# Six gate and up places and eight down places, four weight loads under way, and the last two pairs of experts interleaved

## What is computed

```python
def _hierarchical_moe(xt, w_rg, b_rg, w_re, b_re, w_gate, w_up, w_down):
    ...
    combine = jnp.sum(jax.nn.one_hot(expert_id, N_EXPERTS, dtype=jnp.float32)
                      * (g1 * g2)[..., None], axis=1).astype(xt.dtype)
    y = jnp.zeros_like(xt)
    for e in range(N_EXPERTS):
        he = jax.nn.silu(xt @ w_gate[e]) * (xt @ w_up[e])
        y = y + combine[:, e:e + 1] * (he @ w_down[e])
    return y
...
        x = x + y.reshape(B, T, D)
    return _rmsnorm(x, final_norm)
```

## Time and profile before

| | us |
|---|---|
| runs, median of 3 | 1471.9 |
| runs, lowest and highest | 1466.81, 1473.19 |
| profiled execution | 1470.25 |
| its span (first to last instruction) | 1468.4 |
| PE, DVE, ACT, POOL busy | 1337.8, 662.8, 505.2, 572.6 |
| weight loads (SP), DMA share of the span on its queue | 35.5% |

### The profile page before, as it was taken

One profiled execution on the slowest core, in us unless ns is written; L12 is line 12 of the kernel. 1 busy time (PEld: TensorE's weight loads), 2 busy tenths in 40 slices (PEclk: granted clock), 3 DMA queues, 4 the chain that ended last, 5 costly groups with the idle time before them and its releaser, 6 DMA issues. The chain is left out here.

```text
span 1468.4 us, 20026 instructions
## 1 busy us (share of the span) xinstructions
PE 1337.8 (91%) x7696; PEld 955.2 (65%) x7696; DVE 662.8 (45%) x1346; ACT 505.2 (34%) x970; POOL 572.6 (39%) x531
## 2 busy tenths in 40 slices
PE   4999999989999899798998999999999889999855
PEld 3767767778878776576888876677767733333222
DVE  5456953257722679624761413443444611111115
ACT  3312333356632423335662433544442111111002
POOL 2113687334444437953436403543342311111125
PEclk9999999999999999889999999999999799999988
DMA  8672111130022311120003212211036959999993
GB/s 336 269 283 100 44 44 44 43 129 1 2 90 90 113 58 58 44 86 15 1 2 102 72 58 86 87 58 44 29 143 242 368 210 394 358 371 371 376 346 153
DMA packets 42652, 210.06 MB, mean 143 GB/s; under 512 B 7271, under 2 KB 9703, under 8 KB 33328
## 3 DMA queue, kind: packets, MB, share of 16 engines
q1 hardware_dynamic: 34336, 195.11, 35.5%
q0 software_dynamic: 5760, 10.27, 1.9%
q10 hardware_dynamic: 2448, 3.21, 0.7%
HBM read 201.98 MB, written 17.30 MB: 149 GB/s over the span
## 5 line engine op out<-in xcount | busy, mean ns | idle before, releaser
L425 POOL TENSOR_TENSOR wlo<-raw,whi 128x1024 fp32r<-128x1024 f32 x57 | 139.4, 2447 | 107.0 <-ACT whi L413 73.6
L3260 PE MATMUL ps<-gu,XT 128*64 128x512 f32 x608 | 136.7, 595 | 6.9 <-DVE XT L3360 4.2
L853 PE MATMUL ps<-hxh,whi 128*128 128x512 f32 x304 | 131.6, 433 | 5.7 <-ACT whi L413 5.7
L853 PE MATMUL ps<-hxh,wlo 128*128 128x512 f32 x304 | 124.0, 408 | 13.8 <-POOL wlo L425 13.8
L1115 DVE SCALAR_TENSOR_TENSOR z<-glu,small,z 128x798 f32<-128x798 f32 (+1 forms) x120 | 129.1, 1127 | 0.7
L853 PE MATMUL ps<-hxl,whi 128*128 128x512 f32 x304 | 122.4, 403 | 0.0
L3260 PEld LDWEIGHTS ps<-gu,XT 128*64 128x64 f32 x608 | 46.5, 137 | 84.1 <-issue 73.1
L1618 POOL TENSOR_SCALAR P<-P,stat 128x768 f32<-128x768 f32 (+1 forms) x80 | 65.5, 821 | 84.6 <-DVE stat L1580 83.5
L3285 PE MATMUL ps<-dn,heT 128*64 128x512 f32 x304 | 78.5, 626 | 21.8 <-issue 12.4
L1462 PE MATMUL ps<-kT,qT 96*128 96x256 f32 (+1 forms) x432 | 91.7, 348 | 3.8 <-ACT P L1516 2.1
L1516 ACT ACTIVATE P<-ps,stat 128x768 f32<-128x768 f32 (+1 forms) x80 | 65.1, 814 | 63.2 <-DVE stat L1573 62.6
(11 more groups left out here) (844 smaller groups left out, 3173.3 us busy)
## 6 DMA issues: line engine op xcount, KB each, us to landing
gu<-in_w_gu_dram SPq DMA_DIRECT2D x32, 2048.0 KB, 10.0
raw<-in_w_in_dram SPq DMA_DIRECT2D x66, 512.0 KB, 3.4
dn<-in_w_dn_dram SPq DMA_DIRECT2D x32, 1024.0 KB, 7.6
wgate<-in_w_mod_dram SPq DMA_DIRECT2D x16, 1024.0 KB, 8.5
raw<-in_w_out_dram SPq DMA_DIRECT2D x24, 512.0 KB, 3.3
wmod<-in_w_mod_dram SPq DMA_DIRECT2D x4, 2048.0 KB, 13.6
ybuf<-zero SPq DMA_DIRECT2D x1, 4096.0 KB, 12.0
yin<-ybuf SPq DMA_DIRECT2D x4, 1024.0 KB, 10.0
```

The source lines that it names most:

```text
L425: e.tensor_tensor(K.lo[i][:, :], K.raw[i % 2][:, :], K.hi[i][:, :].bitcast(F32), ALU.subtract).then_inc(*q.up("lo", i))
L853: p = e.matmul(s[0:m, o:o + n], a, K.h[l, v][x][:, k, :], start=k == 0 and part == 0 and x == 0, stop=end)
L3260: m = e.matmul(s[o, :], x[:, k, o], gu[:, k, :], start=k == 0, stop=k == KT - 1, skip_group_check=True)
```

## The change

- There are 6 gate and up places and 8 down places, and the list of first loads has 14 entries, the last five (gu3, gu4, dn6, gu5, dn7) after the attention output is done.
- A load waits for the load four ahead of it, not two.
- Pair 14's up goes into the interleaved loop: up 14, down 13, (far jobs), turn of pair 15's rows, turn of he; after the loop up 15, down 14, the first sums, down 15. Its results still become y parts and not scatters. The second XT and the held bank are gone.
- yin, y parts, owner matrices and row2 lie in other weight places that are free by then; far jobs use another he buffer.

```diff
--- before.py
+++ after.py
@@ -24,7 +24,7 @@
-N_GU, N_DN = 7, 6
+N_GU, N_DN = 6, 8
@@ -317,7 +317,7 @@
-      + [(f"dn{i}", 8 * kb, 130, 199) for i in range(N_DN)]
+      + [(f"dn{i}", 8 * kb, 130 if i < 6 else 131, 199) for i in range(N_DN)]
@@ -2550,7 +2550,7 @@
-    last_walk(S, loads=loads, more_loads=lambda: experts_load(S, 4))
+    last_walk(S, loads=loads, more_loads=lambda: experts_load(S, 5))
@@ -2891,7 +2891,7 @@
-    first = ["gu0", "gu1", "dn0", "dn1", "gu2", "dn2", "dn3", "dn4", "dn5", "gu3", "gu4", "gu5", "gu6"]
+    first = ["gu0", "gu1", "dn0", "dn1", "gu2", "dn2", "dn3", "dn4", "dn5", "gu3", "gu4", "dn6", "gu5", "dn7"]
@@ -2914,14 +2914,14 @@
-    return after("last") + [("x_out", 1, T2 - 1, 1)] * (w == "gu" and x > 2)
+    return after("last") + [("x_out", 1, T2 - 1, 1)] * (x > (2 if w == "gu" else 5))
...
-        for s in q(*weight_free(w, x), *([("w", *EXPERT_LOADS[i - 2])] if i > 1 else [])):
+        for s in q(*weight_free(w, x), *([("w", *EXPERT_LOADS[i - 4])] if i > 3 else [])):
@@ -2934,14 +2934,14 @@
-    last = PAIRS - 3
-    E.w_gu, E.w_dn = weight_place(K, "gu", 2 * PAIRS), weight_place(K, "dn", 2 * last)
-    E.row2 = sb("row2", [128, D], F32, f"dn{(2 * last + 1) % N_DN}")
-    E.yin = [sb(f"yin{t}", [128, 2, D], F32, f"gu{(2 * last + t // 2) % N_GU}", 8192 * (t % 2)) for t in range(T2)]
-    E.x2 = sb("XT2", [128, KT, 128], F32, f"dn{(2 * last + 1) % N_DN}", 4096)
...
+    last = NE - 6
+    at = lambda w, x: f"{w}{x % (N_GU if w == 'gu' else N_DN)}"
+    E.w_gu, E.w_dn = weight_place(K, "gu", last), weight_place(K, "dn", last)
+    E.yin = [sb(f"yin{t}", [128, 2, D], F32, at("gu", last + t // 2), 8192 * (t % 2)) for t in range(T2)]
+    E.parts = [[sb(f"y{j}{p}", [128, D], F32R, at("dn", (last + 1, last - 2)[j]), 4096 * c) for c, p in enumerate("hl")] for j in range(2)]
+    E.owner = [sb(f"own{j}", [128, T2, 128], F32R, at("dn", last - 1), 2048 * j) for j in range(4)]
+    E.row2 = sb("row2", [128, D], F32, "Y")
@@ -3077,36 +3077,13 @@
-    for i in range(PAIRS - 2):
...
-    lower(i)
-    second_stored(i)
-
     def far(n):
...
-        upward(job, "XT", 0)
-        downward(job, 0, y)
+        upward(job, "XT", 1)
+        downward(job, 1, y)
@@ -3115,13 +3092,37 @@
-    guarded(everyone, farther(0), all_far)
+    p, last = PAIRS - 2, PAIRS - 1
+    turned(("first", 0), ("xg", 0), "XT")
+    first_gather(2)
+    for i in range(last):
+        job, job2 = ("first", i), ("second", i)
+        upward(job, "XT", 0)
+
+        def more_up():
+            turned(job2, "xg2", "XT")
+            upward(job2, "XT", 1 + i % 2)
+        if i < p:
+            guarded(numbers, crowded(i), more_up)
+        load(loads_of("gu", i))
+        if i < p:
+            turned(("first", i + 1), ("xg", (i + 1) % 2), "XT")
+        if i + 1 < p:
+            second_gather(i + 1)
+        first_gather(i + 3)
+        if i:
+            lower(i - 1)
+            second_stored(i - 1)
+        if i == p:
+            guarded(everyone, farther(0), all_far)
+            turned(("first", last), ("xg", 1), "XT")
+        turn_up(job, 0, free("heT"))
+        free.set(("he", 0), ev("he_turned", job))
...
-    free.at["part", 0], free.at["part", 1] = free(("Y", 0)) + free(("Y", 1)), end
+    free.at["part", 0] = free.at["part", 1] = end
@@ -3156,18 +3157,14 @@
     owner(0, "pool", end)
     owner(2, "pool", end)
-    turned(("first", p), ("xg", 0), "XT")
-    upward(("first", p), "XT", 0)
-    downward(("first", p), 0, None, 0)
-    free.at["x2"] = end
-    turned(("first", last), ("xg", 1), "x2")
-    hold_up(("first", last))
+    upward(("first", last), "XT", 0)
+    down(("first", p), None, 0, free(("part", 0)))
+    free.set("heT", ev("down", ("first", p), 1))
     guarded(numbers, crowded(p), lambda: own_second(p, 1))
...
     taken_in(0)
-    upward(("first", last), "x2", 0)
     begin_sum(0)
     begin_sum(1)
```

More of the change, by code:

```diff
@@ L2936, in experts_buffers @@
     E.heT = sb("heT", [128, 2, 128], F32, "he", 3072)
-    last = PAIRS - 3
-    E.w_gu, E.w_dn = weight_place(K, "gu", 2 * PAIRS), weight_place(K, "dn", 2 * last)
-    E.row2 = sb("row2", [128, D], F32, f"dn{(2 * last + 1) % N_DN}")
-    E.yin = [sb(f"yin{t}", [128, 2, D], F32, f"gu{(2 * last + t // 2) % N_GU}", 8192 * (t % 2)) for t in range(T2)]
-    E.x2 = sb("XT2", [128, KT, 128], F32, f"dn{(2 * last + 1) % N_DN}", 4096)
-    place = f"gu{2 * PAIRS % N_GU}"
-    E.parts = [[sb(f"y{j}{p}", [128, D], F32R, *((place, 4096 * c) if j else ("Y", 4096 * (1 - c)))) for c, p in enumerate("hl")] for j in range(2)]
-    E.owner = [sb(f"own{j}", [128, T2, 128], F32R, place, 8192 + 2048 * j) for j in range(4)]
+    last = NE - 6
[5 more added lines that the diff above has]
+    E.row2 = sb("row2", [128, D], F32, "Y")
     E.ms2, E.rs2 = K.stat[:, 64:68], K.stat[:, 72:76]
@@ L3007, in lists, with experts_walk @@
     return [("list",), *[("h2d", t) for t in range(T2)]]
-def experts_walk(S, engine, empty2=nothing, gather=nothing, load=nothing, turn_x=nothing, hold_up=nothing, up=nothing, turn_up=nothing, down=nothing,
+def experts_walk(S, engine, empty2=nothing, gather=nothing, load=nothing, turn_x=nothing, up=nothing, turn_up=nothing, down=nothing,
                  scatter=nothing, stored=nothing, far_load=nothing, rows_in=nothing, owner=nothing, add=nothing, to_x=nothing, rows_sum=nothing,
@@ L3079, in lower @@
         load(loads_of("dn", i))
-    turned(("first", 0), ("xg", 0), "XT")
-    first_gather(2)
-    for i in range(PAIRS - 2):
-        job, job2 = ("first", i), ("second", i)
-        upward(job, "XT", 0)
[L3086 to L3099, removed]
-    lower(i)
-    second_stored(i)
     def far(n):
@@ L3117, in all_far @@
             guarded(everyone, farther(n), lambda: far(n))
-    guarded(everyone, farther(0), all_far)
+    p, last = PAIRS - 2, PAIRS - 1
[23 more added lines that the diff above has]
+        free.set(("he", 0), ev("he_turned", job))
     end = free("heT")
-    p, last = PAIRS - 2, PAIRS - 1
     second_gather(p)
     rows_in(end, free(("Y", 0)) + free(("Y", 1)))
-    free.at["part", 0], free.at["part", 1] = free(("Y", 0)) + free(("Y", 1)), end
+    free.at["part", 0] = free.at["part", 1] = end
     for t in range(T2):
@@ L3131, in own_second @@
         turned(job, "xg2", "XT")
-        upward(job, "XT", 0)
-        downward(job, 0, None, 1)
+        upward(job, "XT", 1)
+        downward(job, 1, None, 1)
         for t in range(T2):
@@ L3246, in turn_x @@
                     m.then_inc(*q.up(*ev("x_turned", job, c)))
-    def hold_up(job):
-        held[job] = K.bk.hold(*ev("he", job))
     def up(job, xt, j, free):
-        s, before = held[job] if job in held else take(*ev("he", job))
-        x, ws = E.x2 if xt == "x2" else E.XT, weights_of(K, E, job)
+        s, before = take(*ev("he", job))
+        x, ws = E.XT, weights_of(K, E, job)
         n = 128 // len(ws)
@@ L3262, in up @@
                     m.then_inc(*q.up(*ev("up", job)))
-        if job in held:
-            K.bk.release(*ev("he", job))
     def turn_up(job, j, free):
@@ L3305, in add @@
                 K.bk.release(*name)
-    experts_walk(S, "pe", turn_x=turn_x, hold_up=hold_up, up=up, turn_up=turn_up, down=down, add=add)
+    experts_walk(S, "pe", turn_x=turn_x, up=up, turn_up=turn_up, down=down, add=add)
 def experts_act(S):
@@ L3314, in turn_x @@
     def turn_x(job, buf, xt, free):
-        x = E.x2 if xt == "x2" else E.XT
+        x = E.XT
         for w in q(ev("x_turned", job, 1), *free):
```

## The result

| | before | after |
|---|---|---|
| median, us | 1469.36 (1466.41 to 1473.19, 4 runs) | 1448.64 (1447.80 to 1451.45, 4 runs) |
| ratio | | 0.9861, 95% interval 0.9829 to 0.9892 |
| profiled execution, span | 1470.25, 1468.4 | 1447.80, 1446.0 |

The change takes 20.7 us off, where the forecast had 12 and a time of 1459 us. In the traced executions the spans differ by 22.4 us.

The account below looks back on a forecast made before the run. From 1195 us the expert weights' DMA stream, then the work after its last landing, was taken to bound the kernel. Gains of 7 us from the rate and 5 from the order gave 1459 us, range 1451 to 1467.

Parts of the forecast that it names:

- What bounds: Expert stage, from 1195 us: the weights still to come set the end, then the work after the last of them.
- W: Expert stage: the landing of the last weight, dated at 1429 us before and forecast at 1422 after.
- Places, 0: Weight places, 7 and 6 becoming 6 and 8: nothing won or lost, the stretch before 1195 staying as it is.
- Four under way, 7.1 us: Weight stream from 1195: four loads under way raise DMA share from 0.96 to 0.99, winning 7.1 us, bounds 0 and 9.4.
- Rival (3): Weight stream and end: all comes back, share 0.998 and no slow clock, yin loads earlier: 1453 us; chance 0.10.
- The rule on HBM: Weight stream: HBM side binds at about 358 GB/s a core, so four under way would win 0; the prediction held it contradicted.
- The order, 5 us: Last two pairs: up 14 before down 13 and up 15 before down 14 win about 5 us.
- Down 15 at W + 11: Last pair: its down matmuls start at 1433.0 instead of 1444.87, 11 us after the last weight instead of 15.9.
- rival (4): Expert stage, result buffer Y0: rows starve as scatters slow beside more queued weights; slower, 1491 us; chance 0.05.
- The yin loads, covered by 1.4 us: End: yin loads wait for pair 13's scatter; VectorE's 1.2 us take-in ends at 1430.6, copy of he due at 1432.
- Slow clock, 1.5 us: Up 15, after TensorE's wait for gu31: a lower granted clock adds 1.5 us, bounds 0 to 7.
- From the last down to the end, 23.5 us: End of the kernel: the same work in the same order follows the last down, 23.5 us.

Follow-up runs that it names:

- E1: The kernel before with each weight load waiting for the load four ahead instead of two, old places and order kept: 1457.65 us, ratio 0.9921.
- E7: The changed kernel with the old order of the last two pairs put back, new places and four loads under way kept: 1458.27 us, ratio 0.9943.
- E2: The changed kernel with two weight loads under way again instead of four, new places and order kept: 1463.65 us, ratio 0.9956.
- E4: The changed kernel with two Y result buffers used in turn by the first jobs instead of one: 1445.99 us, ratio 0.9845.
- E6: The changed kernel with two Y buffers in turn and six weight loads under way instead of four: 1445.4 us, ratio 0.9847.
- E9: The changed kernel with each weight load as two halves over all 128 partitions, a half waiting for the half three ahead: 1472.65 us, ratio 1.0018.
- E10: The changed kernel with each weight load as two halves over all 128 partitions, a half waiting for the half eight ahead: 1443.31 us, ratio 0.9816.
- E5: The changed kernel with each weight load as two halves of 64 partitions, a half waiting for the half three ahead: 1644.25 us, ratio 1.1199.
- E8: The kernel before with four weight loads under way and two Y buffers used in turn: 1454.85 us, ratio 0.9911.
- E11: The changed kernel with two Y buffers in turn and pair 15's turn of he and down ahead of the first sums: 1445.72 us, ratio 0.9840.
- E12: The changed kernel run again, unedited, in the same series as E9 to E11: 1448.74 us, ratio 0.9852.

## Why the prediction was wrong, point by point

- **What bounds: right.** E1, which changes the gate alone, moves the end by 10 us. The dating of W (1429) holds by the packets too.
- **Places, 0: right.** E7 has them and E1 not, and the two are alike. The share ahead of 1195 was 0.25 (0.23 before), and the first load after it began at 1194.4 (1195 before).
- **Four under way, 7.1 us with bounds of 0 and 9.4: the step that failed.** The share reached the 0.99 that was forecast. But the sum took the missing 4% of busy share for the whole loss, as if a busy engine always moved the same. It moved 371 / 0.96 = 386 GB/s for a full share before and 408 / 0.99 = 412 after. The share's three points are the 7 us forecast; the other 14 of the 21 come from the 7% by which a full share moved more (86.8 MB at 0.99 x 386 are 227 us, at 0.99 x 412 213), which is that packets took less time: from 1222 to 1372 those of 8 KiB 0.346 us on the mean before and 0.311 after, those of 16 KiB 0.656 and 0.621. The rows to see it were there: 398 / 0.98 = 406 in the first stretch and 430 / 1.00 in the short one of the earlier trace rows, against 386 for the whole. The prediction took both to be the same ceiling and costed the share alone, so its upper bound was no bound. Rival (3), all comes back, failed in the same term: it priced "all" at 2.3 us more.
- **The rule on HBM** (the Trainium skill, DMA: Bandwidth & Descriptors, Where 436 GB/s comes from), by which about 358 GB/s a core would bind: contradicted by 425 and 416 GB/s over 150 us, not just by 398 over 27. All runs here use one core alone; what holds beside other cores at work no run shows.
- **The order, 5 us: near alone, too small together.** At gate 2 order and places gave 4.1 us in the medians (E2). In its trace the way from W to the last down was 3.3 us shorter than before (12.6 against 15.9), not 4.9, the wait for Y being there too. At gate 4 it gave 11 to 12 (the 20.7 of the whole less the 9.0 of E7 or the 10.1 of E1), because early weights leave the old order's last two pairs standing behind down 13, where W no longer sets the end. The prediction took both parts as terms to add, each measured from W.
- **Down 15 at W + 11: wrong by 3.6 us.** It began at W + 14.6. The step "down 13 to 1409.9, rows of pair 15 and the turn of he to 1411.4" put nothing between down 13 and the turn. In the trace stand there the write to Y0, which waits for a scatter, and a branch behind it. The mechanism is that of rival (4), at a small part of its price: ACT waited for ybuf 9 times from 1222 on instead of 4 times, which the prediction had named as the sign against it. Turns of Y0 with such a wait took 10.6 to 16.8 us, a pair's weights 17.2 (SyncE's issues, 1347.17 to 1364.39), so none before the last held the weights up. E4 takes the wait away, its last down comes at W + 9.0, and its time is 1 to 3 us less.
- **The yin loads, covered by 1.4 us: the loads right, the cover not.** GpSimd's first sum began at 1414.90, 7.1 us after W; the forecast had 5 (1427 against 1422). But the take-in was not 1.2 us long. It began at 1418.85, ahead of the copy of he, and ran beside GpSimd's sums:

```profile
1418.85 3.17 DVE L3393 TENSOR_TENSOR xN<-xN,yin 128x1024 f32<-128x1024 f32 x1 [0.31 <-DVEq L2995]
1421.94 0.41 DVE L3362 COPY heT<-ps 128x256 f32<-128x256 f32 x1
```

  The copy of he waited for it, and TensorE for the copy, 1.31 us ahead of the last down, where it is 0.52 with the copy free (E4): 0.8 us lost, by a slower instruction, not by a later scatter. The copy is free in E4 because its take-in (1416.94, 1.23 us) was done before GpSimd's next sum began at 1417.50.
- **Slow clock, 1.5 us: about right.** In 1400.2 to 1407.0, after TensorE had stood idle for 5.24 us, the granted clock was 0.52 (near the lower of its levels, 1.2 GHz), and up 15 took 7.89 instead of 7.09, the turn ahead of it 1.94 instead of 1.09.
- **From the last down to the end, 23.5 us: right** (23.6).
- **Rows and depth.** With two, four and six loads under way the median scatter took 11.5 (E2), 11.2 (E4) and 11.2 us (E6); with halves, whose packets are half as big, 7.9 (E9) and 7.8 (E10), at either depth. So depth costs the rows nothing, and packet size does. The Trainium skill (DMA: Bandwidth & Descriptors, Queues, rings and completion order) says that engines take turns between queues packet by packet; these numbers agree with it, though the turns themselves were not looked at.

Had the rate term been 21 instead of 7.1, and the rest as forecast, the sum would have read 1445. The measured 1448.6 is that plus the 3.6 us by which the last down stood further from W than forecast.

## What to carry to other kernels

Divide GB/s by busy share and compare the quotient between stretches before using a share as the loss: a busy DMA engine need not be moving at its rate. Keep bytes queued, not transfers: here 2 MiB behind each landing gave all but 1.5 us in 76 MiB's time, 1 MiB lost 15 to 22. Before a median of a view is believed, look how many landings it is made of. And when a stream is sped up, look for the serial work that stood behind it, and cost an order and a rate together, since the gain of one hangs on whether the other still sets the end.

## What the runs showed of the hardware that was not expected

- A transfer over 64 partitions ran at half rate: 16 KiB packets took 1.23 us (median) instead of 0.611, and 228 GB/s moved at a share of 0.99 (E5).
- With 1 MiB queued, 7 to 9% of the 8 KiB packets took over 1.15 of their usual time, and the engines counted as busy (the table above).
- A scatter beside weight packets of 16 and 8 KiB took 11.1 to 11.6 us (medians of E1 to E4, E6 to E8, E11 and E12), beside packets of 8 and 4 KiB 7.9 and 7.8 (E9, E10).
- At the end of the list the engines didn't finish together: with nothing left to issue since 1393.1, the share was 0.39 in 1400 to 1408 (after).
- VectorE's addition of 128x1024 took 1.23 us by itself and 3.17 beside GpSimd's additions of the same shape (after, at 1430.50 and 1418.85).
